# A fused transformer, SSM and mixture-of-experts step on one core: stages joined at their seams, and the expert loop written in another order on every engine

## The chip, the core and the metric

The kernel runs on one core of a Trainium2 chip. A core has engines with an instruction stream each: TensorE (PE in the profile; its weight loads are PEld), VectorE (DVE), ScalarE (ACT), GpSimd (POOL) and SyncE (SP), which here only issues DMAs. They share an SBUF of 128 partitions, hand results from PE over in PSUM, and order one another by semaphores. The metric is the device time of one execution, in microseconds (us).

## What is computed

One trunk layer over 9 tiles of 128 tokens (1 tile of a prompt, 8 of a latent grid), of width 1024: projections, convolution, a bidirectional scan and a differential attention, then the part on which the change bears:

```python
x = x + gate1 * mix
h = rms_norm(x, lw['norm_ffn_g']) * (1 + scale2) + shift2
# hier_moe: 4 groups of 4 experts, a token takes the 2 best of its best group
hidden = (jax.nn.silu(jnp.einsum('nd,edf->nef', hf, lw['w_exp_gate']))
          * jnp.einsum('nd,edf->nef', hf, lw['w_exp_up']))
y = jnp.einsum('nef,efd->nd', hidden * combine.astype(hf.dtype)[..., None], lw['w_exp_down'])
x = x + gate2 * hier_moe(h, lw)
y_sample = rms_norm(xs, final_norm_g)
```

There are 16 experts. One has a gate and an up matrix of 1024x256 each and a down matrix of 256x1024, in float32: 3 MB.

## The kernel before

Stages follow one another: projection, convolution, scan, attention, mixer, routing, expert, final. Each opens a `Scope` with its buffers and semaphores. At a scope's end its semaphores are cleared and all engines meet in a barrier, and no engine starts the next stage before it. Products are made of three matmuls (`split_product`: high·high, high·low, low·high), so each operand has a high part (rounded, a copy on ACT) and a low part (`split_low`, value less high part, line 88).

**Mixer.** For each tile it makes the router's logits (`router(t)`, L1672) and the modulated activations h2 (`modulated(t)`, two DVE instructions of 128x1024, L1666 and L1668), which SP stores to the DRAM scratch `h2` (L1527). `modulated(8)` is the last DVE work of the stage. SP then waits for the stores of all tiles.

**Routing.** It starts with loads, of small tables and of expert 0's weights (SP, L1809 to L1813). DVE ranks experts, counts tokens and builds `entry` and `oh_place`. 36 small matmuls (L1841) turn them into a table of which token goes to which of 33 blocks of 128 slots. Meanwhile DVE works out `past`, `of_block` and the flags that say which block brings in a new expert. At the end it copies the table out of PSUM (`block_token`, L1947). A block belongs to one expert, and blocks 2, 3, 4, 5, 7, 9, 11, 13, 14, 15, 16, 18, 20, 22 and 24 load a new expert's weights; blocks 25 to 32 load none.

**Expert.** The loop runs over the blocks, one `body(t, left)` for each on each engine (`left` counts the blocks that remain). For block t:

- SP issues the loads of the gate/up weights three blocks ahead (`wgu`, 2 MB) and of the down weights two ahead (`wd`, 1 MB), where the block brings a new expert, and stores the outputs (`store`, 512 KB).
- POOL copies the block's 128 token numbers into `idx` (L2037), gathers these rows of h2 from DRAM into `xg` (`gather`, L2040, 512 KB) two blocks ahead, and makes the low part of the down weights (`wd_lo`, 2 instructions of 128x1024).
- PE runs `gate_up(t+1)` (24 matmuls of 512 columns into `gu_ps`), turns the hidden values of t (2 transposes) and the gathered rows of t+2 (8 transposes into `x_ps`), and runs y(t) (12 matmuls of 512 columns into `y_ps`).
- ACT rounds the gate/up weights of t+2 (`gu_high`, 4 pieces, L2115), evacuates y(t-1), rounds the down weights of t+1 (`d_high`, L2121), computes silu(t+1) and rounds x(t+2) (`x_high`, L2126).
- DVE makes hidden(t), the low part of the gate/up weights of t+2 (`gu_low`, 4 pieces of 128x1024), the high and low part of the turned hidden values (`hidT_hi`, L2188, and `hidT_lo`), then the low part of x(t+2) (`xT_lo`).

`xT_hi`, `xT_lo`, `hidT_hi`, `hidT_lo`, `x_ps` and `y_ps` exist once. So y(t) on PE waits for hidT(t), which DVE makes while PE turns x(t+2).

**Final.** SP loads three rows, the two gates and the gain, broadcast to 128 partitions (1.5 MB, L2235 and L2236). For each tile POOL copies two columns of `slot_of` into `idx` and gathers two blocks of expert outputs (`ya`, `yb`). DVE adds them, multiplies by the gate, adds to x2 (`residual`, 3 instructions of 128x1024). ACT takes the sum of squares and its root; DVE inverts and refines the root (5 instructions of one column) and writes the normalised tile (L2294), which SP stores. Three buffers of each kind go round.

## Time and profile before

| what | us |
|---|---|
| median of 3 runs | 1359.76 (1357.14 to 1360.11) |
| the profiled execution | 1359.61 |
| its span | 1357.8 |
| mixer's last instruction on DVE to routing's first | 889.0 to 893.7 |
| routing's first to the expert stage's first | 893.7 to 919.95 |
| expert stage's first to y(0) | 919.95 to 949.55 |
| y(0) to y(31) | 949.55 to 1272.80 |
| y(31) to the final stage's first | 1272.80 to 1286.6 |
| final stage | 1286.6 to 1357.8 |

All times are of the profiled execution, from the start of its span. PE is busy in 82% of the span, DVE in 59%, ACT in 48% and POOL in 32%. These shares are means over eight stages with different limits, so each seam and the loop have to be read for themselves: which engine is idle, and which instruction ends its wait.

### The profile page before, as it was taken

How to read it: one execution, taken by the hardware profiler on the slowest of the kernel's cores; microseconds unless marked ns; L12 is line 12 of the kernel's file. 1: busy time of each engine (PE TensorE's matmuls, PEld its weight loads, DVE VectorE, ACT ScalarE, POOL GpSimd, SP SyncE). 2: the span in 40 equal slices, each digit the busy share in tenths (PEclk: the TensorE clock that was granted, in tenths of full speed). 3: DMA queues.
4: the chain of work that ended last, by engine and by line, in shares of the span. 5: the costliest groups of instructions: out<-in, count | busy, mean ns of one | idle time of the engine just before them, and what ended most of it. 6: DMA issues, size and time to landing. Idle time of an engine off the chain costs nothing. (4 is left out here: it accounts for less than half of the span.)

```text
span 1357.8 us, 19140 instructions
## 1 busy us (share of the span) xinstructions
PE 1116.0 (82%) x5908; PEld 934.1 (69%) x5908; DVE 799.6 (59%) x1230; ACT 651.5 (48%) x1048; POOL 437.8 (32%) x295
## 2 busy tenths in 40 slices
PE   4899999979885896998995999936999999999600
PEld 1687777759885785988884888835777777777500
DVE  1754543026454585777773567565778667787277
ACT  2641111123232573666665456205868677878322
POOL 0000000030003393466761000003666557576341
PEclk8899999989997897999997999956999999999855
DMA  9418577131001806235003433136876977633274
GB/s 358 166 62 300 193 231 251 55 98 41 16 1 30 203 33 159 53 93 144 32 16 110 142 107 112 47 110 227 287 270 233 351 270 259 225 117 111 86 272 168
DMA packets 127091, 204.90 MB, mean 151 GB/s; under 512 B 19264, under 2 KB 89824, under 8 KB 124974
## 3 DMA queue, kind: packets, MB, share of 16 engines
q1 hardware_dynamic: 118108, 176.90, 39.3%
q0 software_dynamic: 7344, 26.74, 6.1%
q10 hardware_dynamic: 1570, 0.38, 0.2%
q8 instruction: 38, 0.62, 0.2%
q14 instruction: 31, 0.25, 0.1%
HBM read 215.61 MB, written 45.01 MB: 192 GB/s over the span
## 5 line engine op out<-in xcount | busy, mean ns | idle before, releaser
L88 POOL TENSOR_TENSOR moe_wd_lo<-moe_wd,moe_wd_hi 128x1024 fp32r<-128x1024 f32 x66 | 163.5, 2499 | 104.0 <-ACT moe_wd_hi L2121 104.0
L88 DVE TENSOR_TENSOR moe_wgu_lo<-moe_wgu,moe_wgu_hi 128x1024 fp32r<-128x1024 f32 x132 | 173.0, 1371 | 39.9 <-ACT moe_wgu_hi L2115 37.0
L2115 ACT CAST moe_wgu_hi<-moe_wgu 128x1024 fp32r x132 | 128.7, 1051 | 65.6 <-DMA moe_wgu<-in_w_exp_up 65.1
L93 PE MATMUL proj_acc_ps<-proj_w_hi,hidden_hT_hi 128*128 128x512 f32 x288 | 117.8, 409 | 6.7 <-DVE hidden_hT_lo L88 6.7
L95 PE MATMUL proj_acc_ps<-proj_w_hi,hidden_hT_lo 128*128 128x512 f32 x288 | 115.0, 399 | 0.0
L94 PE MATMUL proj_acc_ps<-proj_w_lo,hidden_hT_hi 128*128 128x512 f32 x288 | 114.5, 398 | 0.0
L93 PE MATMUL moe_gu_ps<-moe_wgu_hi,moe_xT_hi 128*128 128x512 f32 x264 | 106.2, 402 | 4.7 <-DVE moe_xT_lo L88 4.7
L1278 POOL TENSOR_TENSOR att_e<-att_e 128x1152 f32<-128x1152 f32 (+1 forms) x36 | 86.1, 2391 | 74.1 <-DVE att_e L1345 74.1
L94 PE MATMUL moe_gu_ps<-moe_wgu_lo,moe_xT_hi 128*128 128x512 f32 x264 | 105.7, 400 | 0.0
L95 PE MATMUL moe_gu_ps<-moe_wgu_hi,moe_xT_lo 128*128 128x512 f32 x264 | 105.6, 400 | 0.0
L1296 ACT ACTIVATE att_e<-att_sc_ps,att_shift 128x1152 f32<-128x1152 f32 (+1 forms) x72 | 81.5, 1132 | 39.4 <-DVE att_shift L1334 39.2
L650 POOL MEMSET conv_ones<- 128x128 f32 x1 | 0.2, 205 | 281.4 <-POOLq L83 281.4
L1334 DVE TENSOR_REDUCE att_shift<-att_sc_ps 128x1 f32<-128x1152 f32 (+1 forms) x72 | 86.0, 1230 | 4.3 <-PE att_sc_ps L1375 4.2
L1404 PE MATMUL att_turned_ps<-att_in_v_tok,att_aT 128*128 128x128 f32 x584 | 77.5, 280 | 8.4 <-ACT att_aT L1304 8.3
L1404 PEld LDWEIGHTS att_turned_ps<-att_in_v_tok,att_aT 128*128 128x128 f32 x584 | 69.9, 191 | 14.7 <-ACT att_aT L1304 11.2
L93 PEld LDWEIGHTS proj_acc_ps<-proj_w_hi,hidden_hT_hi 128*128 128x128 f32 x288 | 54.8, 190 | 26.3 <-DVE hidden_hT_lo L88 7.1
L93 PE MATMUL moe_y_ps<-moe_wd_hi,moe_hidT_hi 128*128 128x512 f32 x132 | 56.6, 429 | 19.8 <-DVE moe_hidT_lo L88 17.6
L93 PE MATMUL conv_group_ps<-hidden_hT_hi,conv_w_hi 128*128 128x384 f32 x192 | 65.5, 341 | 8.7 <-ACT conv_xin L685 8.7
L2121 ACT CAST moe_wd_hi<-moe_wd 128x2048 fp32r x33 | 63.0, 1909 | 5.1 <-DMA moe_wd<-in_w_exp_down 5.1
L95 PE MATMUL conv_group_ps<-hidden_hT_hi,conv_w_lo 128*128 128x384 f32 x192 | 64.9, 338 | 0.0
L94 PE MATMUL conv_group_ps<-hidden_hT_lo,conv_w_hi 128*128 128x384 f32 x192 | 64.8, 338 | 0.0
L95 PEld LDWEIGHTS proj_acc_ps<-proj_w_hi,hidden_hT_lo 128*128 128x128 f32 x288 | 54.7, 190 | 13.3
(353 smaller groups left out, 2716.6 us busy)
## 6 DMA issues: line engine op xcount, KB each, us to landing
moe_wgu<-in_w_exp_gate SPq DMA_DIRECT2D x34, 1024.0 KB
moe_wgu<-in_w_exp_up SPq DMA_DIRECT2D x34, 1024.0 KB
moe_wd<-in_w_exp_down SPq DMA_DIRECT2D x34, 1024.0 KB
scratch_y_slots<-moe_y SPq DMA_DIRECT2D x33, 512.0 KB
proj_raw<-in_w_in SPq DMA_DIRECT2D x32, 256.0 KB, 4.8
proj_feat<-in_w_ada SPq DMA_DIRECT2D x4, 2048.0 KB, 8.7
proj_xh<-in_w_ada SPq DMA_DIRECT2D x4, 2048.0 KB, 9.6
scratch_h<-mix_h SPq DMA_DIRECT2D x9, 512.0 KB, 2.9
```

Of the source, the lines that this page charges most:

```text
L88: return eng.tensor_tensor(low, value, high.bitcast(F32), ALU.subtract)
L93: pe.matmul(out, a_high, b_high, start=start, stop=False)
L94: pe.matmul(out, a_high, b_low, start=False, stop=False)
L95: return pe.matmul(out, a_low, b_high, start=False, stop=stop)
L650: pool.memset(ones[:], 1.0).then_inc(zeroed, 1)
L1278: pool.tensor_tensor(e[:, it.e, 0, 0:it.keys], e[:, it.e, 0, 0:it.keys], e[:, it.e, 1, 0:it.keys], ALU.add).then_inc(a_done, 1)
L1296: act.activation(as_banks(it, e[:, it.e, m, 0:it.keys]), scores_of(it, m), ACT.Exp, bias=shift[:, it.e, m:m + 1], accum_out=total[:, it.e, ...
L1334: dve.tensor_reduce(shift[:, it.e, m:m + 1], scores_of(it, m), AX if it.prompt else AXY, ALU.max, negate=True).then_inc(shift_done[m], 1)
L1404: mm = pe.matmul(o_ps, aT[:, j * P:(j + 1) * P], v_tok[:, j + (0 if it.prompt else 1), it.head * P:(it.head + 1) * P], start=(j == 0), sto ...
L2115: act.copy(wgu_hi[:, k.buf, j:j + 2], wgu[:, buf, j:j + 2]).then_inc(gu_hi_done, 1)
L2121: act.copy(wd_hi[:, k.buf], wd[:, buf]).then_inc(d_hi_done, 1)
```

## The change

In words, in the order of the program:

1. `amul`, `aadd`, `h2` and `rstd2` move from the mixer's scope into one that lasts until routing has ended. The mixer ends with the last tile's logits. Routing's DVE stream runs the last tile's modulation between the last `entry` and `past`, and SP stores its h2 there.
2. In the expert stage the first two gathers take their indices straight from `block_token`; later ones still copy them, and run four blocks ahead. POOL's `d_low` and ACT's `d_high` run two blocks ahead of use rather than on or one block ahead of it, ACT's `gu_high` three ahead.
3. PE's body runs the first half of `gate_up(t+1)`, then the transposes of t's hidden values and of x(t+2), then the second half of `gate_up(t+1)`, then y(t). `x_high`, `x_low` and their semaphores go by halves.
4. ACT's body is in the order x_high(t+2), silu(t+1), gu_high(t+3), with evacuate(t) in its middle, and d_high(t+2). DVE's body is hidT(t), the last piece of gu_low(t+2), x_low(t+2), hidden(t+1), and three pieces of gu_low(t+3).
5. SP loads the final stage's three rows when one block is left, into half of the weights' buffer.
6. The final stage is unrolled, with four buffers for the gathers, which read their indices straight from `slot_of`. Roots are inverted and refined for two tiles at once: five times rather than nine.
7. Two semaphores live longer than a stage (`h2_in`, `final_in`), and their scopes have something to clear when they close.

```diff
+def modulate(dve, W, t):
+    h2, x2, cond = W["h2"][:, t % 2], W["x2"][:, t], 0 if t == 0 else 1
+    dve.scalar_tensor_tensor(out=h2, in0=x2, scalar=W["rstd2"][:, t % 2:t % 2 + 1], in1=W["amul"][:, cond], op0=ALU.mult, op1=ALU.mult)
+    dve.drain()
+    return dve.tensor_tensor(h2, h2, W["aadd"][:, cond], ALU.add)
...
-            store_h2(TILES - 1)
-            sp.wait_ge(h2_stored[0], 16 * 5)
-            sp.wait_ge(h2_stored[1], 16 * 4)
+            for u in range(2):
+                sp.wait_ge(h2_stored[u], 16 * 4)
...
-            modulated(TILES - 1)
+            dve.wait_ge(h2_stored[(TILES - 1) % 2], 16 * ((TILES - 1) // 2))
...
+            sp.wait_ge(last_done, 1)
+            sp.dma_start(M["h2"][(TILES - 1) * P:, :], W["h2"][:, (TILES - 1) % 2]).then_inc(W["h2_in"], 16)
             sp.wait_ge(w_in, 16 * 3)
+            sp.wait_ge(W["h2_in"], 16)
...
+            modulate(dve, W, TILES - 1).then_inc(last_done, 1)
             tt(past[:], bcast(steps[:], NE, 2), bcast(bend[:], BLOCKS, 1), ALU.is_ge)
...
+                if left == 1:
+                    sp.wait_ge(gu_lo_done, BLOCKS + 2)
+                    load_final_gains(sp, I, W, M)
...
+            def first_gather(k):
+                pool.indirect_dma_start(xg[:, k.buf], None, M["h2"],
+                                        bass.IndirectOffsetOnAxis(ap=token[:, k.n:k.n + 1], axis=0)).then_inc(xg_in[k.buf], 16)
             def gather(k):
                 pool.wait_ge(x_turned, k.n + 1)
                 pool.tensor_copy(idx[k.buf][:], token[:, bass.ds(k.n, 1)]).then_inc(idx_done, 1)
-                pool.wait_ge(idx_done, k.n + 1)
+                pool.wait_ge(idx_done, k.n - 1)
                 pool.sem_inc(started, 1)
                 pool.indirect_dma_start(xg[:, k.buf], None, M["h2"],
                                         bass.IndirectOffsetOnAxis(ap=idx[k.buf][:], axis=0)).then_inc(xg_in[k.buf], 16)
             def body(t, left):
+                if left >= 4:
+                    gather(t.next().next().next().next())
                 if left >= 2:
-                    gather(t.next().next())
-                buf = weight_buffer(pool, t)
-                pool.wait_ge(d_hi_done, t.n + 1)
+                    d_low(t.next().next())
+            def d_low(k):
+                buf = weight_buffer(pool, k)
+                pool.wait_ge(d_hi_done, k.n + 1)
                 for half in range(2):
-                    op = split_low(pool, wd_lo[:, t.buf, half], wd[:, buf, half], wd_hi[:, t.buf, half])
+                    op = split_low(pool, wd_lo[:, k.buf, half], wd[:, buf, half], wd_hi[:, k.buf, half])
                 op.then_inc(d_lo_done, 1)
-            gather(Step(0, 0))
-            gather(Step(0, 1))
+            first_gather(Step(0, 0))
+            first_gather(Step(0, 1))
+            d_low(Step(0, 0))
+            gather(Step(0, 2))
+            gather(Step(0, 3))
+            d_low(Step(0, 1))
             blocks(pool, body)
...
+            def turn_hidden(t):
                 pe.wait_ge(hid_done, t.n + 3)
                 pe.wait_ge(hidT_done, t.n + 1)
                 for j in range(2):
                     mm = pe.transpose(h_ps[:, j * P:(j + 1) * P], hid[:, j * P:(j + 1) * P], ident[:])
                 mm.then_inc(h_turned, 1)
+            def gate_up(k, half):
+                pe.wait_ge(x_lo_done[half], k.n + 2)
+                if half == 0:
+                    pe.wait_ge(gu_lo_done, k.n + 3)
+                    pe.wait_ge(hid_done, k.n + 1)
+                for j in range(half * (KT // 2), (half + 1) * (KT // 2)):
+                    cols = slice(j * P, (j + 1) * P)
+                    mm = split_product(pe, gu_ps[k.buf][:], xT_hi[:, cols], xT_lo[:, cols],
+                                       wgu_hi[:, k.buf, j], wgu_lo[:, k.buf, j], j == 0, j == KT - 1)
+                mm.then_inc(gu_done if half else gu_half_done, 1)
+            def body(t, left):
+                if left >= 1:
+                    gate_up(t.next(), 0)
+                turn_hidden(t)
                 if left >= 2:
                     turn_x(t.next().next())
+                if left >= 1:
+                    gate_up(t.next(), 1)
                 pe.wait_ge(hidT_done, t.n + 2)
...
             turn_x(Step(0, 0))
-            gate_up(Step(0, 0))
+            gate_up(Step(0, 0), 0)
             turn_x(Step(0, 1))
+            gate_up(Step(0, 0), 1)
...
             def body(t, left):
                 if left >= 2:
-                    gu_high(t.next().next())
-                if not (isinstance(t.n, int) and t.n == 0):
-                    evacuate(Step(t.i, t.c - 1))
+                    x_high(t.next().next(), 0)
+                    x_high(t.next().next(), 1)
                 if left >= 1:
-                    d_high(t.next())
                     silu(t.next())
+                if left >= 3:
+                    ahead = t.next().next().next()
+                    buf = weight_buffer(act, ahead)
+                    gu_high(ahead, buf, range(0, KT // 2, 2))
+                evacuate(t)
+                if left >= 3:
+                    gu_high(ahead, buf, range(KT // 2, KT, 2))
                 if left >= 2:
-                    x_high(t.next().next())
-            gu_high(Step(0, 0))
-            x_high(Step(0, 0))
-            gu_high(Step(0, 1))
+                    d_high(t.next().next())
+            gu_high(Step(0, 0), weight_buffer(act, Step(0, 0)), range(0, KT, 2))
             d_high(Step(0, 0))
+            x_high(Step(0, 0), 0)
+            x_high(Step(0, 0), 1)
+            gu_high(Step(0, 1), weight_buffer(act, Step(0, 1)), range(0, KT, 2))
+            x_high(Step(0, 1), 0)
+            x_high(Step(0, 1), 1)
             silu(Step(0, 0))
-            x_high(Step(0, 1))
+            gu_high(Step(0, 2), weight_buffer(act, Step(0, 2)), range(0, KT, 2))
+            d_high(Step(0, 1))
             blocks(act, body)
-            evacuate(Step(0, BLOCKS - 1))
...
             def body(t, left):
-                hidden(t)
-                if left >= 2:
-                    gu_low(t.next().next())
                 dve.wait_ge(h_turned, t.n + 3)
                 dve.wait_ge(y_done, t.n + 2)
                 dve.tensor_copy(hidT_hi[:], h_ps[:, 0:FF])
                 dve.drain()
                 split_low(dve, hidT_lo[:], h_ps[:, 0:FF], hidT_hi[:]).then_inc(hidT_done, 1)
                 if left >= 2:
+                    gu_low(t.next().next(), range(KT - 2, KT, 2))
                     x_low(t.next().next())
-            gu_low(Step(0, 0))
+                if left >= 1:
+                    hidden(t.next())
+                if left >= 3:
+                    gu_low(t.next().next().next(), range(0, KT - 2, 2))
+            gu_low(Step(0, 0), range(0, KT, 2))
             x_low(Step(0, 0))
-            gu_low(Step(0, 1))
+            gu_low(Step(0, 1), range(0, KT, 2))
             x_low(Step(0, 1))
+            hidden(Step(0, 0))
+            gu_low(Step(0, 2), range(0, KT - 2, 2))
             blocks(dve, body)
+def final_gains(W):
+    rows = W["wgu"][:, 0].rearrange("p k n -> p (k n)")
+    return [rows[:, c * D:(c + 1) * D] for c in range(3)]
...
+def final_gains(W):
+    rows = W["wgu"][:, 0].rearrange("p k n -> p (k n)")
+    return [rows[:, c * D:(c + 1) * D] for c in range(3)]
...
+def load_final_gains(sp, I, W, M):
+    gate0, gate1, gain = final_gains(W)
+    for cond, gate in enumerate((gate0, gate1)):
+        sp.dma_start(gate, row_bcast(M["mods"][cond, GATE2 * D:(GATE2 + 1) * D])).then_inc(W["final_in"], 16)
+    sp.dma_start(gain, row_bcast(I["final_norm_g"])).then_inc(W["final_in"], 16)
...
-                pool.wait_ge(x3_done, t.n + 1)
-                for c in range(2):
-                    pool.tensor_copy(idx[c][t.buf][:], slot_of[:, t.n, c:c + 1]).then_inc(idx_done, 1)
-                pool.wait_ge(idx_done, t.n * 2 + 2)
-                pool.sem_inc(started, 1)
+            for t in range(TILES):
+                if t >= NB:
+                    pool.wait_ge(x3_done, t - NB + 1)
                 for c, dst in enumerate((ya, yb)):
-                    pool.indirect_dma_start(dst[:, t.buf], None, M["y_slots"],
-                                            bass.IndirectOffsetOnAxis(ap=idx[c][t.buf][:], axis=0)).then_inc(y_in[t.buf], 16)
-            tiles(pool, body)
+                    pool.indirect_dma_start(dst[:, t % NB], None, M["y_slots"],
+                                            bass.IndirectOffsetOnAxis(ap=slot_of[:, t, c:c + 1], axis=0)).then_inc(y_in[t % NB], 16)
         @block.scalar
...
+            def normalise(first, n):
+                r = rstd[:, first:first + n]
+                dve.wait_ge(sq_done, first + n)
                 dve.reciprocal(r, r)
-                refine(dve, r, ssq[:, t.buf:t.buf + 1], 1.0 / D, tmp[:])
-                dve.wait_ge(out_stored[t.buf], t.nth * 16 + 16)
-                dve.scalar_tensor_tensor(out=out[:, t.buf], in0=x2[:, t.n], scalar=r, in1=gain[:], op0=ALU.mult,
-                                         op1=ALU.mult).then_inc(out_done, 1)
-            tiles(dve, body, residual)
+                refine(dve, r, ms[:, first:first + n], 1.0, tmp[:, 0:n])
+                for t in range(first, first + n):
+                    if t >= NO:
+                        dve.wait_ge(out_stored[t % NO], 16 * (t // NO))
+                    dve.scalar_tensor_tensor(out=out[:, t % NO], in0=x2[:, t], scalar=rstd[:, t:t + 1], in1=gain, op0=ALU.mult,
+                                             op1=ALU.mult).then_inc(out_done, 1)
+            for t in range(TILES):
+                residual(t)
+                if t >= 2 and t % 2 == 0:
+                    normalise(t - 2, 2)
+            normalise(TILES - 1, 1)
```

What the change moves is shown at three places, as the order of the instructions on an engine. First PE, within one body of the expert loop, around the transposes (L2086 turns hidden values, L2067 turns x). Before:

```order
L94 MATMUL moe_gu_ps<-moe_wgu_lo,moe_xT_hi 128x512
L95 MATMUL moe_gu_ps<-moe_wgu_hi,moe_xT_lo 128x512
L2086 MATMUL moe_h_ps<-all_ident,moe_hid 128x128 x2
L2067 MATMUL moe_x_ps<-all_ident,moe_xg 128x128 x8
L93 MATMUL moe_y_ps<-moe_wd_hi,moe_hidT_hi 128x512
L94 MATMUL moe_y_ps<-moe_wd_lo,moe_hidT_hi 128x512
```

The same place in the changed kernel:

```order
L94 MATMUL moe_gu_ps<-moe_wgu_lo,moe_xT_hi 128x512
L95 MATMUL moe_gu_ps<-moe_wgu_hi,moe_xT_lo 128x512
L2102 MATMUL moe_h_ps<-all_ident,moe_hid 128x128 x2
L2095 MATMUL moe_x_ps<-all_ident,moe_xg 128x128 x8
L93 MATMUL moe_gu_ps<-moe_wgu_hi,moe_xT_hi 128x512
L94 MATMUL moe_gu_ps<-moe_wgu_lo,moe_xT_hi 128x512
```

Twelve matmuls of `gate_up` now stand between the transposes and y(t). Second DVE, in one body of the loop. Before:

```order
L2179 SCALAR_TENSOR_TENSOR moe_hid<-moe_gu_ps,all_block_weight,moe_act_g 128x256
L1990 ISA
L1990 TENSOR_LOAD all_block_buf
...
L88 TENSOR_TENSOR moe_wgu_lo<-moe_wgu,moe_wgu_hi 128x1024
L2186 REGISTER_ALU
L2188 CAST moe_hidT_hi<-moe_h_ps 128x256
L88 TENSOR_TENSOR moe_hidT_lo<-moe_h_ps,moe_hidT_hi 128x256
L88 TENSOR_TENSOR moe_xT_lo<-moe_x_ps,moe_xT_hi 128x1024
```

And now:

```order
L2237 CAST moe_hidT_hi<-moe_h_ps 128x256
L88 TENSOR_TENSOR moe_hidT_lo<-moe_h_ps,moe_hidT_hi 128x256
L2001 ISA
L2001 TENSOR_LOAD all_block_buf
L2001 ISA x2
L2217 REGISTER_ALU
L88 ISA
L88 TENSOR_TENSOR moe_wgu_lo<-moe_wgu,moe_wgu_hi 128x1024
L88 TENSOR_TENSOR moe_xT_lo<-moe_x_ps,moe_xT_hi 128x512 x2
L2231 ISA
L2231 SCALAR_TENSOR_TENSOR moe_hid<-moe_gu_ps,all_block_weight,moe_act_g 128x256
```

Four pieces of `wgu_lo` stood before `hidT`; now `hidT` is first, one piece stands behind it, and three more come after `hid`. Third POOL, where the expert stage starts. Before:

```order
L2037 COPY moe_idx<-all_block_token 128x1
L2040 DMA moe_xg<-scratch_h,moe_idx 128x1024
L2037 COPY moe_idx<-all_block_token 128x1
L2040 DMA moe_xg<-scratch_h,moe_idx 128x1024
L2037 COPY moe_idx<-all_block_token 128x1
L2040 DMA moe_xg<-scratch_h,moe_idx 128x1024
```

And now:

```order
L2050 DMA moe_xg<-scratch_h,all_block_token 128x1024 x2
L2001 TENSOR_LOAD all_block_buf
L2001 ISA x2
L88 ISA
L88 TENSOR_TENSOR moe_wd_lo<-moe_wd,moe_wd_hi 128x1024
L88 ISA
L88 TENSOR_TENSOR moe_wd_lo<-moe_wd,moe_wd_hi 128x1024
```

The two copies of indices are gone, and block 0's low part of the down weights comes before the third gather.

## Rows read from the trace of the kernel before

**Rows 1.** Timeline of DVE, mixer's end and routing: start, us, instruction, [idle before, releaser].

```profile
886.28 0.24 DVE L1672 SCALAR_TENSOR_TENSOR moe_in_logits<-mix_lg_ps,mix_rstd,mix_br_add 128x20 f32<-128x20 f32 x1 [1.09 <-PE mix_lg_ps L1748]
...
893.73 0.19 DVE L1858 TENSOR_REDUCE route_gmax<-moe_in_logits 128x9 f32<-128x36 f32 x1 [4.72 <-PEq L83]
...
918.58 0.20 DVE L1947 CAST all_block_token<-route_table_ps 128x33 uint32<-128x33 f32 x1 [3.11 <-PE route_table_ps L1841]
```

**Rows 2.** The page's DMA issues: KB each, median us to landing.

```profile
scratch_h<-mix_h SPq DMA_DIRECT2D x9, 512.0 KB, 2.9
```

**Rows 3.** Timeline of all engines, where the expert stage starts.

```profile
921.07 1.16 POOL L2040 DMA_INDIRECT moe_xg<-scratch_h,moe_idx  x1 [0.93 <-POOL moe_idx L2037]
...
932.25 1.90 ACT L2121 CAST moe_wd_hi<-moe_wd 128x2048 fp32r x1
...
940.88 0.77 PE L93 MATMUL moe_gu_ps<-moe_wgu_hi,moe_xT_hi 128*128 128x512 f32 x1 [2.36 <-DVE moe_xT_lo L88]
...
947.00 4.75 POOL L88 TENSOR_TENSOR moe_wd_lo<-moe_wd,moe_wd_hi 128x1024 fp32r<-128x1024 f32 x2 [6.01 <-ACT moe_wd_hi L2121]
...
949.55 0.50 PE L93 MATMUL moe_y_ps<-moe_wd_hi,moe_hidT_hi 128*128 128x512 f32 x1
```

**Rows 4.** The gather's line: microseconds from issue to landing.

```profile
DMA to landing us min/median/max: 4.2/5.3/8.6
```

**Rows 5.** Windows: length, busy us (instructions) by engine, PEclk, DMA share, GB/s.

```profile
1054.00:1098.00 44.00, 39.59 (x179) 31.74 (x179) 28.34 (x31) 30.98 (x32) 23.69 (x17) 0.96 0.96 341
...
1193.00:1272.80 79.80, 77.29 (x361) 61.87 (x360) 54.16 (x63) 59.83 (x60) 53.96 (x30) 1.00 0.29 96
...
1297.10:1358.00 60.90, 0.00 (x0) 0.00 (x0) 50.35 (x81) 14.27 (x28) 16.90 (x24) 0.50 0.59 207
```

**Rows 6.** Waits in the loop: engine, line, releaser, total us, times, longest.

```profile
ACT moe_wgu_hi L2115 <- DMA moe_wgu<-in_w_exp_up: 39.5, 12, 4.5
...
PE moe_y_ps L93 <- DVE moe_hidT_lo L88: 16.6, 17, 2.0
```

**Rows 7.** Timeline of PE, one body without a weight load, and y(31).

```profile
1261.72 1.04 PE L2067 MATMUL moe_x_ps<-all_ident,moe_xg 128*128 128x128 f32 x8
1262.90 0.50 PE L93 MATMUL moe_y_ps<-moe_wd_hi,moe_hidT_hi 128*128 128x512 f32 x1
1263.24 0.40 PE L94 MATMUL moe_y_ps<-moe_wd_lo,moe_hidT_hi 128*128 128x512 f32 x1
...
1265.81 0.40 PE L93 MATMUL moe_gu_ps<-moe_wgu_hi,moe_xT_hi 128*128 128x512 f32 x1
...
1272.80 0.50 PE L93 MATMUL moe_y_ps<-moe_wd_hi,moe_hidT_hi 128*128 128x512 f32 x1 [1.02 <-DVE moe_hidT_lo L88]
```

**Rows 8.** Timeline of DVE in that body, gu_low undisturbed.

```profile
1255.48 4.62 DVE L88 TENSOR_TENSOR moe_wgu_lo<-moe_wgu,moe_wgu_hi 128x1024 fp32r<-128x1024 f32 x4
```

**Rows 9.** Timeline of DVE and POOL, a body in which both make low parts.

```profile
1186.07 6.64 DVE L88 TENSOR_TENSOR moe_wgu_lo<-moe_wgu,moe_wgu_hi 128x1024 fp32r<-128x1024 f32 x4
...
1188.15 1.20 POOL L2037 COPY moe_idx<-all_block_token 128x1 uint32 x1
...
1191.79 5.55 POOL L88 TENSOR_TENSOR moe_wd_lo<-moe_wd,moe_wd_hi 128x1024 fp32r<-128x1024 f32 x2 [0.48 <-ACT moe_wd_hi L2121]
```

**Rows 10.** Timeline of DVE, final stage.

```profile
1297.18 1.23 DVE L2280 TENSOR_TENSOR fin_ya<-fin_ya,fin_yb 128x1024 f32<-128x1024 f32 x1 [10.41 <-DMA fin_yb<-scratch_y_slots,fin_idx]
...
1300.94 1.22 DVE L2280 TENSOR_TENSOR fin_ya<-fin_ya,fin_yb 128x1024 f32<-128x1024 f32 x1
...
1304.67 0.16 DVE L2291 RECIPROCAL fin_rstd<-fin_rstd 128x1 f32<-128x1 f32 x1
...
1305.88 1.29 DVE L2294 SCALAR_TENSOR_TENSOR fin_out<-moe_in_x,fin_rstd,fin_gain 128x1024 f32<-128x1024 f32 x1
...
1307.09 1.22 DVE L2280 TENSOR_TENSOR fin_ya<-fin_ya,fin_yb 128x1024 f32<-128x1024 f32 x1
```

**Rows 11.** Timeline of DVE, last instruction of the final stage.

```profile
1352.90 1.28 DVE L2294 SCALAR_TENSOR_TENSOR fin_out<-moe_in_x,fin_rstd,fin_gain 128x1024 f32<-128x1024 f32 x1
```

159 lines of the change are left out of this document (68 added, 91 removed).

## The prediction

> **What bounds the kernel now.** I read the seams of the stages first, in the timelines, because a share over the whole span hides them. Between mixer and routing DVE waits 4.72 us behind its last modulation, which ended at 889.01 [rows 1]: that is the landing of h2's last store, 2.9 at the median [rows 2], and about 1.8 of closing a scope. At the end of routing DVE waits again, 3.11 for the table that PE makes [rows 1]. The expert stage opens with a copy of indices (0.93 of wait, [rows 3]), and its first gathers take 4.2 to 5.3 from issue to landing [rows 4]. PE stands still for 2.36 before the second block's gate_up, until xT_lo is there [rows 3].
>
> Then the loop. By the windows it has three faces [rows 5]. From 1193 on, where no block brings weights, PE is busy 77.3 of 79.8 us at full clock with the DMA at 0.29: PE is the bound there, and what is left to gain is small. From 1054 to 1098 the DMA is at 0.96 with 341 GB/s, and PE is idle for a tenth. The waits say the same [rows 6]: 39.5 us of ACT's waits in the loop are for weights, 16.6 of PE's for hidT_lo. In the last stage, 1297 to 1358, PE does nothing, DVE is busy 50.35 of 60.9 [rows 5], and before it DVE waits 10.41 for the first gather [rows 10].
>
> **The sum, part by part**, against the profiled execution of 1359.6, which lies 0.2 under the median.
>
> *Mixer to routing.* The stage would end with the logits at 886.52 (886.28 + 0.24), and the stores of earlier tiles have long landed. With 2.0 for the close (the 1.8 above and a little for the last signal) routing's first DVE instruction comes at 888.5 instead of 893.73: **-5.2**. Bounds: the close could cost 1 more or less, so -4.2 to -6.2.
>
> *The modulation in routing.* It is two instructions, 889.01 less 886.52 or 2.5 us. It stands ahead of `past`, and the whole of that chain ends 3.11 before the table comes [rows 1]. So 0.6 of cover is left: **0**. Its store is issued about 2.5 after the last `entry`; PE's 36 matmuls run longer than store and landing (2.9, [rows 2]) by about a microsecond, so SP's new wait for the landing ends before DVE's last instruction. If that cover is gone, up to 1.5 comes back. Expert 0's loads are issued before SP's new wait, so nothing is queued behind it.
>
> *Expert start.* From the stage's first instruction (921.07 less 0.93 less 0.2, 919.95) to y(0) are 29.6. The first gather goes 1.1 earlier. Against it, d_high(0), 1.9 [rows 3], is now ahead of x_high(0) on ACT; but PE wants only half of x for its first half. Weights landed, ACT is through at 928.3, and half of x_high and half of x_low take about 1.1 more: gate_up(0) starts at 929.4, where it did at 929.9, -0.5. The wait of 2.36 before gate_up(1) is covered by the second half of gate_up(0). Of the -2.9 I take **-2.6**, since hidden(0), which y(0) needs, is behind x_low(1) on DVE now. Bounds: 0 (the third gather or the loads are later) and -4.
>
> *The loop.* y(0) to y(31) took 323.25 (949.55 to 1272.80, [rows 3, 7]), 10.43 a block. In a quiet block: y(30) to y(31) is 9.90. Eleven matmuls of 512 columns follow one another in 2.57 (1263.24 to 1265.81), 0.2335 each. The transposes of x are busy 1.04 and y's first matmul starts 1.18 after their first; it then stands 0.34 until the second, not 0.23 [rows 7]. So about 0.24 is wait for hidT_lo and 0.11 a slow first step. With twelve matmuls (2.8) between the transposes and y, hidT (two DVE instructions, 0.84 in all) is covered, and PE alone would take 9.90 - 0.35 = 9.55 a block.
>
> Can DVE and POOL keep up? Their low parts do not overlap in this trace. Four pieces of gu_low take 4.62 on a free DVE [rows 8], and 6.64 where POOL's d_low is beside them; POOL's pair takes 5.55 there, and a copy of one column stands 1.20 [rows 9]. A pair takes 4.75 when it is alone [rows 3]. A block wants 4.6 + 4.75 + 0.2 for the copy, or 9.5 of PE's 9.55: it just fits, with nothing to spare. The row of 1.20 also says who is next: the copy waited for a whole DVE piece that had been waiting while POOL's half ran. The two take turns. So a piece waits for one half (2.4) at most. The chain that this could hit is: transposes end, hidT 0.9, last gu_low piece 1.15, x_low 1.25, so 3.3 after the transposes; PE needs it after twelve matmuls of gate_up and twelve of y, 5.6. Slack 2.3, one half costs 0.1. Therefore I put the quiet block halfway between the clean 9.55 and today's 9.90, at 9.72.
>
> The Trainium skill, page "SBUF — State Buffer", section "Who interferes with whom", speaks against this change: a DVE instruction with two SBUF inputs and a GpSimd instruction that reads SBUF exclude each other for the whole instruction. It does not say who goes next, which the copy above does. By its rule alone, with both halves in a row allowed to go first, the chain would be 4.7 late rather than 2.4, which is the slower rival below; the trace agrees with the exclusion.
>
> Blocks with weights: gather, store and a load of 3 MB make 4.2 MB, a block without a load 1.05 MB. From block 11 to 18 six of eight load: 27.3 MB, at 341 GB/s 80 us, 10.0 a block. No reordering goes below that there; I put it as four blocks at 10.3 and four at 9.72. Longer lookahead (gathers four ahead, low parts two or three) makes the rest behave like quiet blocks. Sum: 26 at 9.72 (252.7), four at 10.3 (41.2), and the last period, 36 matmuls and two transposes without x, 8.7: 302.6, against 323.25: **-20.6**. Bounds: all thirty at 9.55, -28.0; thirty at 10.25, -7.1.
>
> *y(31) to the final stage:* the same instructions in the same chain, and SP's three loads of rows lie beside PE's work: 0.
>
> *Final start.* DVE's first add comes 10.5 after the stage's start [rows 10]. The copies of indices and the 1.5 MB ahead in the queues are gone. What stays is the issue of two gathers, about 1.3 until the second, and its landing, 5.3 as in the loop [rows 4]: 6.6, **-3.9**. Bounds: -5.0 (landing 4.2) and -0.6 (landing 8.6).
>
> *Final DVE.* Nine residuals at 3.76 (1297.18 to 1300.94) stay. An inversion with its refinement takes 1.21 (1304.67 to 1305.88), and five in place of nine save 4.8. The output takes 1.21 (to 1307.09) nine times. 33.8 + 6.0 + 10.9 = 50.7, where it was 57.0 (1297.18 to 1354.18, [rows 10, 11]): **-6.4**, of which 1.6 is gaps at the loop's turns that I expect gone. Bounds: -4.8 and -7. Gathers and stores are 14 MB in 57 us, 248 GB/s, below the 341 that [rows 5] show: the DMA does not bind.
>
> *Closing two more scopes* at the end: routing to expert shows about 1.1 for one, which includes the stage's start. I take **+1.2** for two; bounds 0 and +2.2.
>
> Sum: -5.2 - 2.6 - 20.6 - 3.9 - 6.4 + 1.2 = -37.5, so 1359.6 - 37.5 = **1322**.
>
> **Rivals.**
> - *PE alone is the bound.* All blocks at 9.55, -28.0 in the place of -20.6: 1315. For it: PE is busy 97% from 1193 on. Against: the 9.5 of 9.55 for the low parts, and the weights' windows. 0.17.
> - *The shared path of DVE and POOL leaves holes.* Low parts fit only if neither ever waits for ACT's high parts. With holes the block goes to about 10.2, near today's mean of 10.43: 30 x 10.2 + 8.7 = 314.7, -8.6 instead of -20.6: 1334. For it: 6.64 for 4.62 and 31 blocks of it. 0.24.
> - *The seams do not give.* The close waits for h2's store as before (5.2 back) and the first final gather lands in 8.6 instead of 5.3: 1322.1 + 5.2 + 3.3, 1331. 0.05.
> - *Slower.* POOL goes twice in a row at the last gu_low piece, in every block, and all of DVE's work is serial with it: DVE 4.6 + 1.2 + 0.5 + 0.8, 7.15, and POOL 4.75, 11.9 a block. 30 x 11.9 + 8.7 = 365.7, +42.4: 1385. It decides from a mean of 11.05 a block, where the 16.9 of the other terms are eaten up. Against it: the copy of 1.20. 0.03.
>
> **How the numbers follow.** The forecast's own case, blocks between 9.6 and 10.0, has 0.51 and 1316 to 1331. The range from 1313 to 1335 takes in the clean case and most of the holes (a block up to 10.25), and leaves out about 0.1 to 0.15. A measurement of this kernel tells 0.2% from no change, 2.7 us. All cases but the last are far below that: faster 0.96, same 0.01, slower 0.03.
>
> **What would show it.** Routing's first DVE instruction at 888.5, and its wait for the table down from 3.1 to 0.6. y(0) 27.0 after the expert stage's start. PE without a wait ahead of y, and blocks at 9.7 where no weights come; the wait for weights on ACT well below 39.5. DVE's first add 6.6 after the final stage's start and 50.7 to its last output. Wrong would be: PE waits for xT_lo or wgu_lo in most blocks (the holes), the wait for the gather instead of hidT_lo ahead of the transposes, or the gathers of the final stage behind each other so that DVE waits between tiles.

## The result and the profile after

| | before | changed |
|---|---|---|
| median us | 1359.43 (1357.14 to 1360.11, 4 runs) | 1344.72 (1335.67 to 1345.51, 4 runs) |
| the profiled execution | 1359.61 | 1345.51 |
| its span | 1357.8 | 1343.8 |

The ratio is 0.9875, with a 95% interval of [0.9852, 0.9899]: 15 us faster, where 37.5 were forecast. The profiled execution of the changed kernel is the slowest of its four; the fastest took 1335.67. Of all executions reported below one is left out: one of the four of d_low_dve took 4308.8, where the other three took 1372.4 to 1377.6. Where the two profiled executions differ, stretch by stretch:

| stretch | before | changed | difference | forecast |
|---|---|---|---|---|
| start to the mixer's last logits | 886.52 | 889.00 | +2.5 | 0 |
| last logits to routing's first on DVE | 7.21 | 1.99 | -5.2 | -5.2 |
| routing's first to its table (L1947, now L1956) | 24.85 | 24.85 | 0 | 0 |
| on to the expert stage's first (POOL) | 1.37 | 2.02 | +0.7 | in the +1.2 |
| expert stage's first to y(0) | 29.6 | 26.3 | -3.3 | -2.6 |
| y(0) to y(31) | 323.3 | 325.1 | **+1.8** | **-20.6** |
| y(31) to the final stage's first | 13.9 | 12.2 | -1.7 | 0 |
| its first to the first add | 10.5 | 7.3 | -3.2 | -3.9 |
| first add to last output | 57.0 | 50.6 | -6.4 | -6.4 |
| last output to the end | 3.6 | 4.5 | +0.9 | in the +1.2 |

The seams did what was worked out for them. The loop did not. The +2.5 ahead of the mixer's end has nothing to do with the change: 2.1 of it are there when the projection ends, in code that is the same, and other executions of that code end the mixer anywhere from 885.1 to 889.3.

The timeline of DVE in the changed kernel, at the seam and in routing, answers [rows 1]:

```profile
888.77 0.24 DVE L1676 SCALAR_TENSOR_TENSOR moe_in_logits<-mix_lg_ps,late_rstd,mix_br_add 128x20 f32<-128x20 f32 x1 [1.20 <-PE mix_lg_ps L1752]
891.00 0.19 DVE L1866 TENSOR_REDUCE route_gmax<-moe_in_logits 128x9 f32<-128x36 f32 x1 [1.99 <-PEq L83]
...
909.68 1.28 DVE L1476 SCALAR_TENSOR_TENSOR late_h<-moe_in_x,late_rstd,late_amul 128x1024 f32<-128x1024 f32 x1
911.03 1.23 DVE L1478 TENSOR_TENSOR late_h<-late_h,late_aadd 128x1024 f32<-128x1024 f32 x1
...
915.85 0.19 DVE L1956 CAST all_block_token<-route_table_ps 128x33 uint32<-128x33 f32 x1 [0.62 <-PE route_table_ps L1849]
```

The wait of 4.72 is 1.99, the two modulation instructions stand in routing, and the wait for the table has shrunk from 3.11 to 0.62: they were hidden, just. The windows of the loop answer [rows 5] (length, busy us by engine PE, PEld, DVE, ACT, POOL, then PE's clock, DMA share, GB/s), up to y(23), from there to y(30), and four microseconds to which we come:

```profile
944.10:1193.90 249.80, 228.84 (x1058) 182.26 (x1059) 215.56 (x209) 184.24 (x209) 183.41 (x93) 0.97 0.77 270
1193.90:1260.60 66.70, 66.70 (x324) 54.32 (x323) 62.03 (x63) 56.14 (x63) 54.02 (x27) 1.00 0.28 103
...
994.00:998.00 4.00, 4.00 (x14) 3.07 (x13) 4.00 (x3) 0.74 (x1) 3.21 (x2) 0.57 0.86 270
```

In the quiet blocks PE is busy 66.7 of 66.7: 9.5 a block, better than the 9.72 of the forecast. Up to y(23), where weights come, PE stands 21 of 250 us, and DVE is busy 216 of them. The waits of the changed loop answer [rows 6] (engine, line, releaser, total us, times, longest):

```profile
ACT moe_wgu_hi L2150 <- DMA moe_wgu<-in_w_exp_up: 28.0, 14, 3.6
...
PE moe_gu_ps L93 <- DVE moe_xT_lo L88: 14.6, 7, 3.6
PEld moe_y_ps L93 <- DVE moe_hidT_lo L88: 11.6, 11, 1.4
PEld moe_gu_ps L93 <- issue: 11.0, 10, 4.0
PEld moe_gu_ps L93 <- DVE moe_wgu_lo L88: 8.5, 4, 4.0
PE moe_y_ps L93 <- DVE moe_hidT_lo L88: 7.0, 10, 0.9
```

The wait for hidT_lo fell from 16.6 to 7.0, as meant. In its place PE waits 14.6 for xT_lo, in 7 waits, the longest 3.6. Three blocks took 15.0, 15.8 and 16.0 us, y(4) to y(5), y(8) to y(9) and y(21) to y(22). This is the first of them in the timeline of all engines:

```profile
985.35 1.14 POOL L2058 DMA_INDIRECT moe_xg<-scratch_h,moe_idx  x1 [0.80 <-POOL moe_idx L2055]
...
986.04 0.42 DVE L88 TENSOR_TENSOR moe_hidT_lo<-moe_h_ps,moe_hidT_hi 128x256 fp32r<-128x256 f32 x1
...
986.51 4.71 POOL L88 TENSOR_TENSOR moe_wd_lo<-moe_wd,moe_wd_hi 128x1024 fp32r<-128x1024 f32 x2
...
986.90 5.42 DVE L88 TENSOR_TENSOR moe_wgu_lo<-moe_wgu,moe_wgu_hi 128x1024 fp32r<-128x1024 f32 x1 [0.43 <-issue]
...
992.24 1.27 DVE L88 TENSOR_TENSOR moe_xT_lo<-moe_x_ps,moe_xT_hi 128x512 fp32r<-128x512 f32 x2
```

POOL starts the pair of d_low at 986.51, 0.02 after its gather. DVE starts the last piece of gu_low 0.4 later, and it takes 5.42 instead of 1.2: both halves of POOL, 4.71, go ahead of it. I call this a double turn. The piece is 4.2 late, and x_low with it; PE stands 3.56, in its own timeline:

```profile
989.19 0.39 PE L95 MATMUL moe_y_ps<-moe_wd_hi,moe_hidT_lo 128*128 128x512 f32 x1
993.15 0.50 PE L93 MATMUL moe_gu_ps<-moe_wgu_hi,moe_xT_hi 128*128 128x512 f32 x1 [3.56 <-DVE moe_xT_lo L88]
...
993.95 0.39 PE L93 MATMUL moe_gu_ps<-moe_wgu_hi,moe_xT_hi 128*128 128x512 f32 x1
994.19 0.55 PE L94 MATMUL moe_gu_ps<-moe_wgu_lo,moe_xT_hi 128*128 128x512 f32 x1
994.53 0.63 PE L95 MATMUL moe_gu_ps<-moe_wgu_hi,moe_xT_lo 128*128 128x512 f32 x1
994.96 0.63 PE L93 MATMUL moe_gu_ps<-moe_wgu_hi,moe_xT_hi 128*128 128x512 f32 x1
```

After the 3.56 of idle come four matmuls that take 0.39 to 0.50, then one of 0.55 and seven of 0.63, which start 0.43 after one another and no longer 0.23. The granted clock is 0.50 from 994.27 to 997.68, the lower of its two levels (1.2 GHz of 2.4); the window above, at 0.57, holds most of that. In the second block the lower level stands from 1035.23, before PE goes on at 1036.50, until 1042.06. So a double turn in this profile costs 3.6 of idle, 1.5 of slow matmuls (2.2 in the second block, with eleven steps of 0.43), and a wait for hidT behind it: 5.5 to 6.5 us in all, against a block of 9.5.

The three blocks hold 17 of the 23 us by which this loop is longer than that of no_d_low below, up to y(23). The other twenty take 10.15 each.

### The profile page after: what moved, and what is told of

Its sections match the earlier page's. It is cut to its first block and busy times, and to the rows that moved or that the text cites. A ratio compares the mean times of both kernels' runs of the same rounds, so it can differ in the third digit from the quotient of the medians.

```text
span 1343.8 us, 19190 instructions
## 1 busy us (share of the span) xinstructions
PE 1115.2 (83%) x5908; PEld 932.5 (69%) x5908; DVE 847.3 (63%) x1243; ACT 653.7 (49%) x1081; POOL 473.7 (35%) x275
## 5 line engine op out<-in xcount | busy, mean ns | idle before, releaser
L88 DVE TENSOR_TENSOR moe_wgu_lo<-moe_wgu,moe_wgu_hi 128x1024 fp32r<-128x1024 f32 x132 | 225.5, 1745 | 39.2 <-ACT moe_wgu_hi L2150 20.9
L88 POOL TENSOR_TENSOR moe_wd_lo<-moe_wd,moe_wd_hi 128x1024 fp32r<-128x1024 f32 x66 | 190.1, 2902 | 70.7 <-ACT moe_wd_hi L2156 70.5
L2150 ACT CAST moe_wgu_hi<-moe_wgu 128x1024 fp32r x132 | 131.7, 1051 | 52.5 <-DMA moe_wgu<-in_w_exp_up 52.2
L93 PE MATMUL moe_gu_ps<-moe_wgu_hi,moe_xT_hi 128*128 128x512 f32 x264 | 111.4, 422 | 17.1 <-DVE moe_xT_lo L88 17.0
L93 PEld LDWEIGHTS moe_gu_ps<-moe_wgu_hi,moe_xT_hi 128*128 128x128 f32 x264 | 51.4, 195 | 32.9 <-issue 11.0
L93 PEld LDWEIGHTS proj_acc_ps<-proj_w_hi,hidden_hT_hi 128*128 128x128 f32 x288 | 54.8, 190 | 26.3 <-DVE hidden_hT_lo L88 7.1
L95 PEld LDWEIGHTS proj_acc_ps<-proj_w_hi,hidden_hT_lo 128*128 128x128 f32 x288 | 54.7, 190 | 13.5
```

The source lines that it names most:

```text
L88: return eng.tensor_tensor(low, value, high.bitcast(F32), ALU.subtract)
L93: pe.matmul(out, a_high, b_high, start=start, stop=False)
L95: return pe.matmul(out, a_low, b_high, start=False, stop=stop)
L2150: act.copy(wgu_hi[:, k.buf, j:j + 2], wgu[:, buf, j:j + 2]).then_inc(gu_hi_done, 1)
```

## The experiments

All are variants of the changed kernel unless it says otherwise. The columns are the median, that of the kernel before on the same chip in the same job, the ratio with its 95% interval, and from the profile y(0) to y(31), the mean block up to y(23) and from there to y(30), and the longest block. The last period, y(30) to y(31), is shorter (8.6 in the changed kernel), and in neither mean.

| run | us | before | ratio | y0 to y31 | to y23 | to y30 | longest |
|---|---|---|---|---|---|---|---|
| before | 1359.4 | | | 323.3 | 10.61 | 9.90 | 11.8 |
| changed | 1344.7 | 1359.4 | 0.9875 [0.9852, 0.9899] | 325.1 | 10.86 | 9.52 | 16.0 |
| after_again | 1340.7 | 1360.1 | 0.9843 [0.9820, 0.9866] | 324.5 | 10.55 | 10.46 | 16.0 |
| seams_only | 1347.8 | 1362.5 | 0.9892 [0.9875, 0.9909] | 325.8 | 10.72 | 9.90 | 12.1 |
| expert_only | 1350.5 | 1362.5 | 0.9905 [0.9875, 0.9936] | 322.4 | 10.74 | 9.53 | 16.2 |
| no_d_low | 1321.3 | 1362.5 | 0.9697 [0.9675, 0.9720] | 301.9 | 9.86 | 9.50 | 12.0 |
| no_loads | 1320.3 | 1362.5 | 0.9677 [0.9648, 0.9707] | 302.1 | 9.86 | 9.53 | 16.1 |
| drain_first | 1428.5 | 1360.1 | 1.0495 [1.0478, 1.0513] | 411.6 | 13.33 | 13.54 | 15.0 |
| drain_between | 1343.4 | 1360.1 | 0.9879 [0.9858, 0.9901] | 326.4 | 10.85 | 9.75 | 13.8 |
| spacer | 1347.1 | 1358.3 | 0.9919 [0.9887, 0.9951] | 324.9 | 10.76 | 9.81 | 13.1 |
| both_wait | 1335.5 | 1360.1 | 0.9811 [0.9795, 0.9828] | 323.5 | 10.50 | 10.47 | 16.1 |
| behind_next | 1349.8 | 1359.6 | 0.9928 [0.9912, 0.9945] | 329.7 | 10.71 | 10.68 | 11.0 |
| quarters | 1353.2 | 1359.6 | 0.9943 [0.9926, 0.9960] | 338.6 | 11.10 | 10.68 | 16.4 |
| split_d_low | 1337.9 | 1358.3 | 0.9837 [0.9809, 0.9864] | 317.1 | 10.50 | 9.56 | 12.3 |
| d_low_dve | 1376.4 | 1359.6 | 1.0127 [1.0107, 1.0148] | 352.2 | 11.46 | 11.28 | 13.5 |
| d_low_dve_1 | 1342.1 | 1358.3 | 0.9866 [0.9838, 0.9894] | 321.4 | 10.58 | 9.91 | 12.5 |

**The two parts apart: seams_only and expert_only.** The first is the changed kernel with the expert stage of before (and the load of the final rows, which the final stage needs); the second is the kernel before with the changed expert stage, without that load:

```diff
 def body(t, left):
     if left >= 3:
         load_gu(t.next().next().next())
-    if left == 1:
-        sp.wait_ge(gu_lo_done, BLOCKS + 2)
-        load_final_gains(sp, I, W, M)
```

> The changed kernel with the expert stage of before (its order on all engines, its gathers with copied indices), the three rows of the final stage still loaded ahead. Theory 1 (the seams gave all of the gain, the loop none of it): by the two traces -5.2 mixer to routing, +0.7 routing's close, about -3.2 final start, -6.4 final DVE, +0.9 end, -13.2 in all, 1346. Theory 2 (seams and loop each gave half, and one of them only looks small by chance): 1350 to 1353.

> The kernel before with the expert stage of the changed one, nothing else. Theory 1 (quiet blocks gain 0.4 each, but in some blocks POOL takes both halves of d_low ahead of DVE's last gu_low piece, PE stands 3.6 us and then works at half clock): quiet blocks 9.5, 1 to 3 blocks of 15 to 16, and a time of 1352 to 1359 which depends on how many such blocks there are. Theory 2 (the long blocks come from the weights' loads): long blocks at the same places as in the changed kernel (5, 9, 22), as the loads are the same.

seams_only: -14.8 against before on that chip, and its stretches are those of the changed kernel (2.0 from logits to routing, 7.2 to the first add, 50.6 to the last output); its expert stage needs 30.1 to y(0), so the first gathers' 3.3 belong to the other part. Against the kernel before that is a little more than the 13.2 of its theory 1. expert_only: -12.1, where its expectation had -1 to -8. Its profiled execution (1355.5, the slowest of four from 1346.1) has y(0) to y(31) in 322.4, with two blocks of 16. They are y(15) to y(16), where the changed kernel had none, and y(21) to y(22), where it had one, while the other two of the changed kernel are at 9.6 and 11.2 here: the loads, which are the same, don't fix them. Its spread of 9 us, and that of the changed kernel, 10, is the size of one or two such blocks.

The two parts do not add up: -14.8 and -12.1 make -26.9, and the changed kernel has -14.7 (-19.4 in after_again). So seams_only does not prove that the loop gives nothing in every execution. Of all three kernels the profile is that of the slowest execution, and none shows what the quickest ones did. Where the missing 8 to 12 us go is open.

**The two suspects taken away: no_d_low and no_loads.**

```diff
 first_gather(Step(0, 1))
+pool.memset(wd_lo[:].bitcast(F32), 0.0)
+pool.drain()
...
-    op = split_low(pool, wd_lo[:, k.buf, half], wd[:, buf, half], wd_hi[:, k.buf, half])
+    op = split_low(pool, wd_lo[:, k.buf, half, 0:8], wd[:, buf, half, 0:8], wd_hi[:, k.buf, half, 0:8])
```

```diff
-dve.tensor_tensor(fresh[:, 1:], of_block[:, 1:], of_block[:, 0:BLOCKS - 1], ALU.not_equal)
+dve.tensor_tensor(fresh[:, 1:], of_block[:, 1:], of_block[:, 1:BLOCKS], ALU.not_equal)
```

> The changed kernel; POOL's low part of the down weights is 8 columns of each half in place of 1024, the rest is cleared once: that part of the products is left out. Theory 1: POOL holds nothing for long, so no DVE piece over 1.4 us, no block over 12, y(0) to y(31) 300 to 306 in place of 325, 1322 to 1327. Theory 2 (loads): the blocks of 15 to 16 stay, y(0) to y(31) over 318, 1338 or more.

> The changed kernel without the experts' weight loads in the loop: all blocks use expert 0's weights, that part of the computation is changed. Theory 1: blocks of 9.5 nearly throughout, y(0) to y(31) 294 to 300, since POOL is never late without late weights, but one block of 15 can still come; 1313 to 1320. Theory 2 (loads make the long blocks): all at 9.5, no long one, 294, 1313. If long blocks are as frequent as with loads (three), lateness of POOL has another source.

no_d_low leaves out most of one of the three products of the down matrix, and no_loads uses expert 0's weights in all blocks. Both came out as theory 1 has it, no_loads with a loop 2 us above its range. Without POOL's low parts, and with all loads, the loop takes 301.9, within a microsecond of the 302.6 that the forecast put, and no DVE piece is over 1.3 us. These are its waits of PE, all small:

```profile
PEld moe_y_ps L93 <- DVE moe_hidT_lo L88: 10.5, 12, 2.8
PE moe_y_ps L93 <- DVE moe_hidT_lo L88: 5.3, 7, 2.3
...
PE moe_gu_ps L93 <- DVE moe_xT_lo L88: 0.4, 1, 0.4
```

The 14.6 for xT_lo are 0.4. ACT's wait for weights is still 33.9 there, so the weights by themselves cost PE little. Without loads, and with all of POOL's work, there is one block of 16.1 and every other is at 9.5 to 9.6, apart from the first (10.3). Thirty blocks of 9.5 and a last period of 8.6 would be 293.6. Loads alone cost 8 over that, low parts alone 8.5, and both together 31.5. I read this so: the loads make ACT late, this makes POOL late, and a late POOL meets DVE at the piece that PE waits for. That both are needed is measured; the chain between them is read from waits, since no run makes ACT alone late, and no_loads takes the traffic of the weights away as well.

**Why POOL goes twice: after_again, drain_between, drain_first, spacer.** In the profiles so far, POOL's first half had started 0.02 after the gather each time that both halves went ahead.

> The changed kernel once more, word for word, for its spread and a second profile. In the profiles so far POOL took both halves of d_low ahead of a waiting DVE piece three times in 325 us, each time with the first half right behind the gather (0.02 us), never where a wait or 0.3 us lay between. Theory 1 (each such turn costs 5.5 to 6.5 us and their number changes from run to run): times between 1325 (none) and 1347 (three), in steps, and a profile whose number of 15 to 16 us blocks explains its time. Theory 2 (the number is fixed by the weights): three again, at the same blocks.

> The changed kernel; POOL drains between the two halves of each d_low. Theory 1 (the second half goes ahead of the waiting DVE piece because it is issued before the first has ended): the DVE piece goes first each time, no piece over 4 us, no long block, 1323 to 1330, and the pair at most 0.1 longer. If who goes next does not hang on when the second half is issued: long blocks as before, up to 1346.

> The changed kernel; POOL drains after each gather, so that d_low's first half can't follow it at once. Theory 1a (POOL takes both halves only when the first one is issued right behind the gather): gap over 0.1 before each first half, no DVE piece over 4 us, no long block, 1323 to 1330. Theory 1b (it happens whenever POOL is late, the gap is only a sign of that): long blocks stay, 0 to 3 of them, 1327 to 1346.

> The changed kernel; after each gather POOL copies one column into a spare tile and waits for it, about 1 us, so that d_low's first half never follows the gather at once. In six profiles all eight cases in which POOL took both halves ahead of a waiting DVE piece had 0.02 between gather and first half. Theory 1a (this is what makes it take both): no DVE piece over 4 us, no block of 15, 1325 to 1336. Theory 1b (the gap is only a sign that POOL is late): POOL is 1 us later still, 1 to 4 long blocks, 1340 to 1350.

```diff
 # drain_between, in d_low
+    if half == 1:
+        pool.drain()
     op = split_low(pool, wd_lo[:, k.buf, half], wd[:, buf, half], wd_hi[:, k.buf, half])
 # drain_first, at the end of gather
+pool.drain()
 # spacer, at the end of gather
+pool.tensor_copy(spare[:], token[:, 0:1]).then_inc(spaced, 1)
+pool.wait_ge(spaced, k.n - 1)
```

after_again has two double turns, at y(4) to y(5) and y(23) to y(24), the second in a stretch that was quiet in the first profile. The first of them makes a block of 13.2 only: PE stands 2.95 and the granted clock stays at 1.00. Another block, y(7) to y(8), takes 13.2 without one. Its four runs are at 1335.9 to 1342.5, and its profile does not explain them: it is the slowest of them, and with one double turn fewer than the first profile its loop is only 0.6 shorter (324.5 for 325.1). Theory 1's steps are not there.

In drain_between no DVE piece took over 4 us, and in spacer none either, with first halves at least 0.83 behind what stood before them. So a second half that is issued late lets DVE go first, and a first half that does not follow the gather at once never brought the second with it. The profiles of the changed kernel, after_again, expert_only, no_loads and both_wait have 145 pairs at whose first half's end a piece of gu_low was waiting. In 16 the pair had followed the gather at 0.02, and in 9 of these both halves went first (one more than the expectation of spacer counts); of the other 129, with 0.1 or more between, none did so. Starting right behind the gather is needed, and not enough. Within the 16 there is a second sign: all 8 whose DVE piece started 0.39 to 0.56 behind the pair were double turns, and of the 8 with 0.64 to 2.2 one was. Why is open.

But the time did not come back, and that is the main lesson of these two: loops of 326.4 and 324.9, without a double turn, for 325.1 with three. Both variants also make POOL later, so they don't tell what double turns alone cost. In spacer two of the seven quiet blocks are at 9.5 and five at 9.8 to 10.0. POOL is a microsecond later there, and its pair starts just ahead of the piece, which then takes up to 3.2:

```profile
1227.82 3.00 DVE L88 TENSOR_TENSOR moe_wgu_lo<-moe_wgu,moe_wgu_hi 128x1024 fp32r<-128x1024 f32 x1 [0.52 <-issue]
```

```profile
1227.35 5.74 POOL L88 TENSOR_TENSOR moe_wd_lo<-moe_wd,moe_wd_hi 128x1024 fp32r<-128x1024 f32 x2 [0.84 <-POOL moe_spare L2061]
```

Those up to y(23) take 10.8. The drains showed something else: on POOL, one behind a gather holds the next instruction until the gather has landed. In drain_first the pair starts 4.82 after the gather's 1.90, without a releaser in the profile:

```profile
1114.65 1.90 POOL L2058 DMA_INDIRECT moe_xg<-scratch_h,moe_idx  x1 [0.80 <-POOL moe_idx L2055]
1121.37 5.70 POOL L88 TENSOR_TENSOR moe_wd_lo<-moe_wd,moe_wd_hi 128x1024 fp32r<-128x1024 f32 x2 [4.82 <-issue]
```

The landing of this gather is recorded 5.53 after its start, and the pair starts 1.2 behind it. drain_between shows it more sharply: in all 15 loop bodies whose gather's landing is recorded, the second half starts 0.25 after that landing, whether this is 4.6 or 8.2 after the gather's start. With it the block is 13.5 in drain_first (1426.5 to 1430.5 us), and in drain_between the second half comes up to 4.9 us behind the first, not 0.1, so the time of its theory 1 missed by 13. So drain_first settles nothing on turns: it measured the drain.

**Another place or another grain: both_wait, behind_next, quarters.**

```diff
 # both_wait, in d_low(k)
+pool.wait_ge(gu_lo_done, k.n + 3)
 # behind_next, in d_low(k), where a gu_low(k + 1) follows
+pool.wait_ge(gu_lo_done, k.n + 4)
 # quarters
 for half in range(2):
-    op = split_low(pool, wd_lo[:, k.buf, half], wd[:, buf, half], wd_hi[:, k.buf, half])
+    for q in range(2):
+        cols = slice(q * 512, (q + 1) * 512)
+        op = split_low(pool, wd_lo[:, k.buf, half, cols], wd[:, buf, half, cols], wd_hi[:, k.buf, half, cols])
```

> The changed kernel; d_low(t+2) on POOL waits, ahead of its first half, until DVE has finished gu_low(t+2), that is its last piece in body t. Theory 1 (the port in front of that piece is what PE waits for): no DVE piece of that kind waits, no PE idle over 1.5 us ahead of gate_up, no block of 15, y(0) to y(31) 298 to 308, 1322 to 1330. Theory 2 (POOL's work has only been moved: DVE's three other pieces and hidT come late instead, since the sum of 9.5 has no slack): blocks of 10.0 to 10.5, 1335 to 1345.

> The changed kernel; POOL's d_low(t+2) waits until DVE has finished the last piece of gu_low(t+3), so that its pair starts behind the piece that PE waits for, not beside it (waiting for gu_low(t+2) changed little, as POOL runs a body behind DVE). Theory 1 (collisions at this piece are the cost): the piece never waits, only the three that follow do, no long block, quiet blocks 9.5, y(0) to y(31) 300 to 310, 1322 to 1330. Rival (the port has no room: 9.5 of 9.5): DVE falls behind in every block, hidT and the next last piece are late, blocks of 10.0 to 10.5, 1335 to 1345.

> The changed kernel with each half of d_low in two instructions of 512 columns, four in all on POOL, 1.2 us each. Theory 1 (a DVE piece waits for what POOL has started, and in some cases for the next one too): waits of 1.2, or 2.4 where two go first, PE idle ahead of gate_up under 1.2, y(0) to y(31) 305 to 315, 1325 to 1335. Rival (POOL keeps the port through all its queued instructions): pieces of over 4 us as before and 1340 to 1346.

both_wait has the lowest ratio of the variants that compute everything, 0.9811, and in its profile, which is of its slowest run, one double turn with a block of 16.1. The reason given for it was wrong: in its trace gu_low(t+2) is done at least 2.3 us before POOL starts d_low(t+2), so the collision stays. Why it is 5 us below after_again in the same job is not shown; their ranges overlap (1333.5 to 1340.8, and 1335.9 to 1342.5).

behind_next does what both_wait was meant to do, and it is the rival of its expectation that came true. The piece that PE waits for never waits (1.23), no block is long, and the blocks take 10.4 to 11.0, 10.7 in the mean with and without loads, a little above that rival's range:

```profile
1212.05 1.23 DVE L88 TENSOR_TENSOR moe_wgu_lo<-moe_wgu,moe_wgu_hi 128x1024 fp32r<-128x1024 f32 x1 [0.51 <-issue]
...
1214.78 6.64 DVE L88 TENSOR_TENSOR moe_wgu_lo<-moe_wgu,moe_wgu_hi 128x1024 fp32r<-128x1024 f32 x3
1221.34 0.41 DVE L2239 CAST moe_hidT_hi<-moe_h_ps 128x256 fp32r<-128x256 f32 x1
```

The three pieces now take turns with POOL's pair, 6.64 instead of 3.5. In the quiet part DVE starts one hidT 10.65 or 10.74 after the other. The wait has moved from x_low to hidT, and PE waits there.

quarters was to make a wait 1.2. It made 8 pieces wait 5.6 to 5.7, and the loop 13.5 slower than in the changed kernel:

```profile
973.91 5.59 DVE L88 TENSOR_TENSOR moe_wgu_lo<-moe_wgu,moe_wgu_hi 128x1024 fp32r<-128x1024 f32 x1 [0.53 <-issue]
```

The rival of its expectation holds, with a time 7 above its range: a waiting piece can stand through the rest of POOL's queue, here four instructions. All 8 are low parts that followed a gather at 0.02, of 10 that did so at 0.02 to 0.04. A copy of one column that follows on POOL gets behind DVE again, as in before.

**Less on the shared path: split_d_low, d_low_dve, d_low_dve_1.** In split_d_low POOL makes half 1 of d_low(t+2) and DVE half 0 of d_low(t+1); in the others DVE makes both halves, of t+2 or t+1, last in its body.

```diff
 # DVE's body in d_low_dve_1 (d_low_dve: if left >= 2: d_low(t.next().next()))
     if left >= 3:
         gu_low(t.next().next().next(), range(0, KT - 2, 2))
+    if left >= 1:
+        d_low(t.next())
```

> The changed kernel with half 1 of d_low on POOL as before and half 0, one block later, as a fifth piece on DVE at its body's end. The shared path wants 4.6 + 1.15 + 2.4 or 8.2 of a block's 9.5 in place of 9.5, and POOL has one instruction to put ahead of a DVE piece, not two. DVE works 8.3. Theory (exclusion with no slack is what costs): no DVE piece over 3.5, quiet blocks 9.5, y(0) to y(31) 298 to 308, 1320 to 1328. Rival (one wait of 2.4 at the wrong piece is enough): blocks of 10 and more wherever weights come, 1330 to 1342.

> The changed kernel with d_low on DVE, two pieces of 128x1024 behind gu_low(t+3) in its body, and nothing but copies of indices and gathers on POOL. DVE then wants 7.15 + 2.3 = 9.45 a block and never waits for the port. Theory 1 (the exclusion is what costs, and it costs twice, since POOL takes 2.4 for what DVE does in 1.15): quiet blocks 9.5 to 9.7, no long block, y(0) to y(31) 300 to 310, 1322 to 1330. Rival (DVE is full, its in-order queue makes hidT late): quiet blocks of 10 or more, 1335 to 1345.

> As d_low_dve, which came out at 11.3 a block, but DVE makes d_low(t+1) in body t, not d_low(t+2), so that its wait for ACT's rounding (36.9 us there) is over before it begins. Theory (the wait for ACT in DVE's queue made it late, not DVE's 9.45 of work): blocks of 9.5 to 9.8, y(0) to y(31) 298 to 306, 1320 to 1328. Rival (DVE is full: handovers and register loads come on top of 9.45): blocks of 10 to 10.6, 1335 to 1350.

split_d_low has the lowest loop of the complete variants, 317.1, and the quiet blocks at 9.56; the longest DVE piece took 2.8. But where weights come it is still at 10.5, not at the 9.9 of no_d_low. So the theory is right on the turns and the quiet blocks, its rival on the rest and on the time, 1337.9. d_low_dve fell on its own order: its waits show DVE held up by ACT, and PE behind it,

```profile
PEld moe_y_ps L93 <- DVE moe_hidT_lo L88: 51.1, 26, 2.3
...
PE moe_y_ps L93 <- DVE moe_hidT_lo L88: 39.7, 26, 1.8
...
DVE moe_wd_lo L88 <- ACT moe_wd_hi L2143: 36.9, 26, 1.7
```

and 11.3 a block, slower than both of its theories. One block later (d_low_dve_1) that wait is gone, DVE's 9.45 of work runs through, and it is at 9.9 in the quiet part, 10.6 in the other, as its rival has it. The 0.5 over the sum of the durations is about what stands between instructions: 15.8 us of "issue" in 26 waits, ahead of wgu_lo. No piece waits for POOL there (none is over 1.25), and the loop is still 19 us above no_d_low: with 9.45 a block, DVE is as full as the shared path was. What remains to shrink is the work itself, and only runs that leave a part of it out show that this gives the time back.

No complete variant beats the changed kernel beyond the scatter of its own two measurements (0.9875 and 0.9843) by much: both_wait is at 0.9811, split_d_low at 0.9837.

## Why the prediction was wrong

The forecast was 1322, in a range from 1313 to 1335; the median is 1344.7. By its own steps:

- *Mixer to routing, the modulation, the final DVE:* right to 0.1 us each. The wait for the table was put at 0.6 and is 0.62. 50.7 was worked out for the final stage's DVE, 50.57 measured.
- *Expert start:* -3.3 for -2.6, within its bounds. *Final start:* -3.2 for -3.9. The first add is 7.3 behind the stage's first instruction. *Closings:* +1.6 for +1.2. It came in two pieces, 0.7 and 0.9, within the bounds. *y(31) to the final stage:* -1.7 where 0 was put; the changed kernel's last evacuation waits for PE and no longer 5 us for a store.
- *Quiet blocks:* 9.5, where 9.55 was worked out for PE alone and 9.72 taken. The slack argument holds there: the last piece takes 1.2 to 2.7, at most one turn, and PE never waits.
- *The loop with weights* is the step that failed: -20.6 was put, and +1.8 measured. "Longer lookahead makes the rest behave like quiet blocks" took the 9.5 of demand on 9.55 as fitting, on average and in the right order. (4.6, 4.75 and 0.2 make 9.55, so by its own numbers nothing was spare.) Up to y(23) the mean is 10.86. A path that is full has no room to take up a late ACT, and ACT waits for weights 14 times, 28.0 us in all. no_loads (302.1) and no_d_low (301.9) show that it takes both. That the second of them comes so near the forecast's 302.6 is luck in part: its quiet blocks are 0.2 better than put, and it has no exclusion to pay for.
- *"So a piece waits for one half (2.4) at most"* was drawn from one row, the copy of 1.20 in [rows 9]. It is wrong. The copy waits for DVE, and that shows who is next behind the pair's second half, but not between the halves. The row that would have shown it, a DVE piece that is already waiting when the first half ends, is not in before's trace: DVE's longest piece there took 3.3, with one half in front of it. What this fault cost by itself is open: spacer and drain_between lose as much without a double turn, but they also make POOL later.
- *The rival "slower"* described this mechanism and its place exactly, POOL twice in a row at the last gu_low piece, 2.4 late. It was priced as if it happened in every block or in none, with a chance of 0.03. It came in three blocks of 31, and each cost 5.5 to 6.5 rather than 2.4. PE's idle time is 3.6, for the piece is 3.3 to 4.2 late, and of the slack of 2.3 no more than 0.7 is left in these blocks; then the granted clock falls to 0.50 for some microseconds. The clock was in no term of the sum, though before's own trace has it: behind a wait of 2.01 for hidT_lo (y(13), 1087.45) its matmuls start 0.43 apart, with the granted clock at 0.50 until 1091.1. In after_again 2.95 of idle left the clock at 1.00.
- *The rival "holes"*, 10.2 a block and 1334, with 0.24, is nearest: the thirty blocks before the last take 10.55 in the mean. It took the holes to be evenly spread, and its block was 0.35 too low.

What was left out of view is that a wait which is hidden in the mean can still come in a few blocks at full length, and then costs more than itself.

The Trainium skill, page "SBUF — State Buffer", section "Who interferes with whom", says that issue order decides who blocks, and that the loser waits for the whole instruction. The traces agree on the exclusion: in all 145 pairs the waiting piece ends 1.08 to 1.12 after the POOL instruction that held it, however long it had waited. They go beyond it: the wait can be for two instructions, and for four in quarters. The prediction had set this against one copy of 1.20, and let the copy decide.

## What to carry to other kernels

When two engines share a path, add up what both want of it in one period; if that is nearly the period, the mean is no forecast. Then ask for each instruction that the bound engine waits for how long it can be held, with the whole queue of the other engine in front of it, and add what the bound engine loses after standing still. Reordering moved the wait (x_low, hidT, ACT) from one place to the next. The time came back where work was left out (no_d_low, no_loads), and a part of it, 8 of 23 us, where half of POOL's work on the path went to DVE (split_d_low). An event that the profile shows clearly, like the double turn, need not be the measure of the loss: take it away alone before it is called the cause.

## What was not expected of the hardware

- Behind a gather, POOL's queued instructions on the shared path can all go ahead of a waiting DVE piece: two of 2.4 (5.42), four of 1.2 (5.7). It happened in 9 of 16 pairs that started 0.02 after a gather (8 of 10 in quarters), and in none of 129 that started later.
- A drain on POOL behind a gather lasts until the gather has landed: in drain_between the next instruction starts 0.25 us after the landing, 15 times of 15, and in drain_first 0.8 to 1.5 after it, with 4.1 us and more of standing still.
- PE's granted clock: after 3.56 us of idle time four matmuls still ran as usual and the lower level came at 994.27, 1.1 us after PE had gone on; after 3.54 us in the second long block it was there 1.3 us before PE went on. It also came behind 2.01 us of idle time in before, and not behind 2.95 in after_again.
